# The last MLP group's down projection as seven block products for 12 of its 16 tiles

## The chip, the cores and the metric

The kernel runs on 1 core of one Trainium2 chip. The metric is the device time of one execution in microseconds, 2284.91 as the median of three (2282.47 to 2286.58).

## The reference

One layer, 512 tokens behind 16 meta tokens, width 2048, all in float32. The change touches only the last lines, the MLP and the final norm.

```python
    h_res = h_res + y
    h = rms_norm(h_res, norm_mlp_g[i])
    h_res = h_res + jnp.square(jax.nn.relu(h @ w_up[i])) @ w_down[i]
out = rms_norm(h_res, final_norm_g)
return out[:, N_META:]
```

`w_up` is 2048 x 8192, `w_down` 8192 x 2048.

## The kernel before

**Tiles.** Activations lie transposed, 128 features on the partitions and 512 tokens along the row; the output of the MLP is 16 tiles of 128 x 512 (`KT`). The hidden width is done in 8 groups of 1024 (`FFG`). A group has an up part (8 hidden tiles, `UT`, made in 4 pairs) and a down part that adds the group's share to all 16 tiles.

**Precision.** Each weight block (128 x 4 x 128, a "quarter") is split into a rounded high part, by ScalarE (`w_hi`), and a low rest, by VectorE (`w_lo`). Each product is three matmuls (`multiply`): high by high, high by low, low by high. Five slots of split blocks run ahead of TensorE (`RM`), and `quarter_used` counts the ones that TensorE is done with.

**Seven products.** In every down but the last, two output tiles (m and m + 8) times two halves of the tokens form a 2 x 2 block problem, and so do the halves of the hidden tiles. Seven products p1, p5, p6, p2, p4, p3, p7 of 12 matmuls with 256 columns take the place of eight. The operands are sums of blocks: `u_form` holds the seven forms of the activation (`uf0`, `uf1`, `uf2`), `w_sum` the sums of weight blocks. ScalarE copies partial results from PSUM to `part`, VectorE combines them into `delta`, and GpSimd adds `delta` to the residual in DRAM (`accum_op`, line 966). The `delta` buffers alternate between two.

**The last group before.** Its ups are made as whole rows (`u_whole`, `u_halves`), without forms. While they run, GpSimd loads the residual back (lines 971 to 973). The down is plain: first 16 tiles over hidden tiles 0 to 3 with 512 columns, then two passes, one for each half of the tokens, over hidden tiles 4 to 7. VectorE evacuates each tile into the residual (`last_res`). Behind each tile of the two passes ScalarE multiplies by the final gain (`nt1`), TensorE turns it (`turn_out`), ScalarE keeps it in `rows`. GpSimd squares each tile and sums the squares (`acc2`, lines 983 and 985), VectorE the last ones. Token sums (`sum_tokens`) give the norm of 256 tokens; the first half's rows are scaled and stored while the second half is still multiplied, the second half's rows at the end.

**What sets the order.** There is no planner: each engine's program is written out, and waits on semaphores link them. The functions: `last_group` on ScalarE and VectorE, the loop over `dense` on TensorE.

Of the kernel before, what the change touches and what calls it, by code (L numbers as in the profile page):

```python
# [31 lines left out]
P = 128  # L32
# [173 lines left out]
ORDER = [t // 2 + HALF_UT * (t % 2) for t in range(UT)]  # L206
# [36 lines left out]
def hybrid_layer(nc, x, meta, norm_mix_g, w_in, shift_mu, conv_w, decay_w0, decay_w2, iclr_a0, iclr_a2,  # L243
# [5 lines left out]
    res_dram = nc.dram_tensor("residual", [D, SEQ], F32, kind="Internal").ap()  # L249
    y_dram = nc.dram_tensor("mixed", [D, SEQ], F32, kind="Internal").ap()  # L250
# [222 lines left out]
    u_sq, u_hi_ready, u_ready = sem("u_sq"), sem("u_hi_ready"), sem("u_ready")  # L473
# [6 lines left out]
    res_back = sem("res_back")  # L480
# [152 lines left out]
    def _(sp):  # L633
# [123 lines left out]

        for m in range(KT):
            load_last(wdn_q[FFG - 1, 0, :, :, m, :], L_UP + m)
        for i in range(2 * KT):  # L760
            load_last(wdn_q[FFG - 1, 1, :, :, i % KT, :], L_UP + KT + i)
        for t in range(4):
            for h in range(2):
                sp.wait_ge(rows_scaled[h], (2, 4, 5, 6)[t])
# [6 lines left out]
    def _(pool):  # L771
# [199 lines left out]
        pool.dma_start(res_a[:], res_view[:, 0:7, :]).then_inc(res_back, 16)  # L971
        pool.dma_start(res_b[:], res_view[:, 7:14, :]).then_inc(res_back, 16)
        pool.dma_start(res_c, res_view[:, 14:16, :]).then_inc(res_back, 16)
        pool.wait_ge(quarter_used, Q_LAST)
        nc.gpsimd.memset(acc2[:], 0.0).then_inc(acc_step, 1)
        steps = ACC_STEPS + 1
        for h in range(2):
            cols = slice(h * NEAR, (h + 1) * NEAR)
            for m in range(KT - 1 - BY_DVE * h):
                n = T_HALF + h * KT + m  # L980
                pool.wait_ge(evacuated[n % 2], free(n))
                pool.wait_ge(acc_step, steps)
                nc.gpsimd.tensor_tensor(psq2[:, cols], last_res(m)[:, cols], last_res(m)[:, cols], ALU.mult).then_inc(acc_step, 1)  # L983
# [8 lines left out]
    def _(act):  # L992
# [396 lines left out]
        def last_group():  # L1389
# [22 lines left out]
            for i in range(2 * KT):  # L1412
# [7 lines left out]
                if i:  # L1420
                    keep_rows(i - 1)
# [1138 lines left out]
```

## Time and profile before

| | |
|---|---|
| median of three | 2284.91 us |
| profiled execution, own time | 2283.76 us |
| its span | 2282.0 us |
| TensorE busy | 2260.2 us, 99% |
| VectorE busy | 1694.0 us, 74% |
| ScalarE busy | 1110.6 us, 49% |
| GpSimd busy | 299.7 us, 13% |
| TensorE clock | 0.999 of full |

The span is the time from the first to the last instruction of one profiled execution. Busy shares are averages over it; which engine counts in a stretch is told by the waits there. PE is TensorE, DVE VectorE, ACT ScalarE, POOL GpSimd, SP SyncE.

### The profile page before, as it was taken

The numbers are of one execution on the slowest core, as the hardware profiler recorded it, in microseconds if no ns is written. First come the engines' busy times: TensorE is split into PE (matmuls) and PEld (weight loads), VectorE is DVE, ScalarE is ACT, GpSimd is POOL, SyncE is SP. The second block draws the span as 40 slices with busy tenths as digits, with TensorE's granted clock in tenths as the row PEclk, the third lists the DMA queues.
The fourth block names the chain that finished last, engine by engine and source line by source line (L and its number), as shares of the span: only waits on it lengthen the run. The fifth ranks groups of instructions, "written<-read, shape, count | busy, mean of one in ns | idle before, by whom it ended". The sixth has DMA issues, their size and how long they took to land.

```text
span 2282.0 us, 50606 instructions
## 1 busy us (share of the span) xinstructions
PE 2260.2 (99%) x19888; PEld 2109.2 (92%) x19888; DVE 1694.0 (74%) x2678; ACT 1110.6 (49%) x2076; POOL 299.7 (13%) x342
## 2 busy tenths in 40 slices
PE   8999999999999999999999999999999999999998
PEld 8999999999999788899999999999999999999888
DVE  7568577577586765588788778788788788787656
ACT  6534444344344423355555545555555455555436
POOL 5102012011020232200100001001001001001007
PEclk9999999999999999999999999999999999999999
DMA  8343343342442562535635636537447447357434
GB/s 253 82 107 83 95 97 85 94 109 70 110 96 81 148 188 81 173 104 136 159 102 138 140 102 157 140 91 166 123 111 167 120 113 170 97 132 196 140 102 153
DMA packets 513306, 286.07 MB, mean 125 GB/s; under 512 B 84526, under 2 KB 490544, under 8 KB 512688
## 3 DMA queue, kind: packets, MB, share of 16 engines
q1 hardware_dynamic: 478512, 224.19, 36.1%
q0 software_dynamic: 24080, 56.20, 11.2%
q10 hardware_dynamic: 10496, 2.62, 0.6%
q8 instruction: 155, 2.54, 0.5%
q14 instruction: 63, 0.52, 0.1%
HBM read 232.47 MB, written 50.47 MB: 124 GB/s over the span
## 4 chain that ended last, share of the span: by engine, by line
PE 91%; DVE 4%; DMA 2%; POOL 1%; ACT 1%; issue 1%; ACTq 0%; SPq 0%; POOLq 0%; DVEq 0%
PE PD L2152 17%; PE PD L2147 11%; PE PD L2402 10%; PE PD L2403 10%; PE PD L2404 10%; PE PW L2402 8%; PE PW L2403 8%; PE PW L2404 8%; PE PD L2368 1%; PE PD L2176 1%; PE PW L2176 1%; POOL acc L985 1%; PE PW L2226 1%; POOL psq L983 1%; DVE w_lo L1550 1%
## 5 line engine op out<-in xcount | busy, mean ns | idle before, releaser
L2152 PE MATMUL PD<-act_both,w_hi 128*128 128x264 f32 (+1 forms) x2496 | 412.7, 287 | 0.0
L2152 PEld LDWEIGHTS PD<-act_both,w_hi 128*128 128x128 f32 x2496 | 341.7, 188 | 11.5 <-issue 6.7
L2403 PE MATMUL PW<-uf,w_hi 128*128 128x256 f32 x1120 | 312.4, 279 | 0.0
L2402 PE MATMUL PW<-uf,w_hi 128*128 128x256 f32 x1120 | 312.4, 279 | 0.0
L2404 PE MATMUL PW<-uf,w_lo 128*128 128x256 f32 x1120 | 312.4, 279 | 0.0
L1036 ACT CAST w_hi<-w_sum 128x512 fp32r<-128x512 f32 x352 | 217.1, 617 | 181.2 <-PE PD L2404 121.2
L1503 DVE TENSOR_TENSOR w_lo<-w_sum,w_hi 128x512 fp32r<-128x512 f32 x352 | 240.4, 688 | 66.9 <-ACT w_hi L1036 65.1
L1550 DVE TENSOR_TENSOR w_lo<-w_raw,w_hi 128x512 fp32r<-128x512 f32 x268 | 200.5, 774 | 97.3 <-ACT w_hi L1052 93.8
L1052 ACT CAST w_hi<-w_raw 128x512 fp32r<-128x512 f32 x268 | 159.1, 619 | 209.4 <-DMA w_raw<-in_w_in 103.1
L2152 PE MATMUL PD<-act_both,w_lo 128*128 128x264 f32 (+1 forms) x1248 | 250.8, 282 | 0.0
L2403 PEld LDWEIGHTS PW<-uf,w_hi 128*128 128x128 f32 x1120 | 210.7, 188 | 0.3
L2402 PEld LDWEIGHTS PW<-uf,w_hi 128*128 128x128 f32 x1120 | 210.6, 188 | 0.3
L2404 PEld LDWEIGHTS PW<-uf,w_lo 128*128 128x128 f32 x1120 | 210.6, 188 | 0.0
L966 POOL DMA_DIRECT2D residual<-form x56 | 66.9, 1195 | 1063.4 <-DVE form L1978 950.6
L2403 PE MATMUL PD<-plain,w_hi 128*128 128x512 f32 x512 | 199.6, 390 | 0.0
L2402 PE MATMUL PD<-plain,w_hi 128*128 128x512 f32 x512 | 199.6, 390 | 0.0
L2404 PE MATMUL PD<-plain,w_lo 128*128 128x512 f32 x512 | 199.3, 389 | 0.0
L2152 PEld LDWEIGHTS PD<-act_both,w_lo 128*128 128x128 f32 x1248 | 191.4, 188 | 0.0
L1503 DVE TENSOR_TENSOR w_lo<-w_more,w_hi 128x512 fp32r<-128x512 f32 x212 | 141.9, 687 | 37.5 <-ACT w_hi L1036 37.3
L1301 ACT ACTIVATE part<-PW 128x256 f32<-128x256 f32 x264 | 101.1, 383 | 135.9 <-PE PW L2404 129.0
L1036 ACT CAST w_hi<-w_more 128x512 fp32r<-128x512 f32 x212 | 126.0, 617 | 67.2 <-PE PD L2404 39.4
L1036 ACT CAST w_hi<-w_raw 128x512 fp32r<-128x512 f32 x180 | 111.1, 618 | 80.6 <-PE PD L2404 36.0
(416 smaller groups left out, 5468.9 us busy)
## 6 DMA issues: line engine op xcount, KB each, us to landing
w_raw<-in_w_in SPq DMA_DIRECT2D x200, 256.0 KB, 3.1
w_raw<-in_w_down SPq DMA_DIRECT2D x136, 256.0 KB, 3.0
w_more<-in_w_down SPq DMA_DIRECT2D x136, 256.0 KB, 3.0
w_raw<-in_w_up SPq DMA_DIRECT2D x128, 256.0 KB, 3.1
w_more<-in_w_up SPq DMA_DIRECT2D x128, 256.0 KB, 3.3
residual<-form POOLq DMA_DIRECT2D x56, 512.0 KB, 7.5
w_raw<-in_w_out SPq DMA_DIRECT2D x64, 256.0 KB, 3.0
residual<-res POOLq DMA_DIRECT2D x2, 2048.0 KB, 10.1
```

The costliest lines, as they stand in the source:

```text
L966: pool.dma_start(res_view[:, p::HALF_KT, :], delta[:, p % 2].rearrange("p (a h) n -> p a (h n)", a=2), accum_op=ALU.add).then_inc(delta_ad ...
L1036: nc.scalar.copy(hi_slot(i), w_sum(SUM_IN[product]) if rel is None else raw_mlp(rel)).then_inc(hi_split, 1)
L1052: nc.scalar.copy(w_hi[:, q % RING], w_raw[:, q % RAW]).then_inc(hi_split, 1)
L1301: nc.scalar.activation(part[:, place, :], bank_for(product, unit) if bank is None else bank, ACT.Copy, scale=scale).then_inc(part_kept, 1)
L1503: V.tensor_tensor(lo_slot(i), w_sum(SUM_IN[product]) if rel is None else raw_mlp(rel), hi_slot(i).bitcast(F32), ALU.subtract).then_inc(lo_ ...
L1550: V.tensor_tensor(w_lo[:, q % RING], w_raw[:, q % RAW], w_hi[:, q % RING].bitcast(F32), ALU.subtract).then_inc(lo_split, 1)
L2147: ins = M(pd_seq(n)[:, 0:width], w, v[:, k, first:first + width], start=begin, stop=end)
L2152: ins = M(PD[:, 2 * (n % 2) + a, cols], w, v[:, k, start:start + cols.stop - cols.start], start=begin, stop=end)
L2176: ins = M(bank[:, h, cols], w, v[:, k, start:start + cols.stop - cols.start], start=begin, stop=end)
L2402: M(bank, whi, hi, start=begin, stop=False, skip_group_check=True)
L2403: M(bank, whi, lo, start=False, stop=False, skip_group_check=True)
L2404: return M(bank, wlo, hi, start=False, stop=end, skip_group_check=True)
```

## The change

The last group's ups go through the same code as the other groups, so that the seven forms are made. Its down is done by seven products for the tile pairs (0, 8) to (5, 13). The tiles 6, 14, 7, 15 (`END_TILES`) stay plain, in 8 steps: four tiles for the first half of the tokens, then four for the second, each over all eight hidden tiles with 256 columns.

Each pair is combined into `delta`, added to the residual in DRAM and loaded back into `res_pair`. Only then can its final gain, its transposes and its squares be made. ScalarE's gains (`gain_rows`) of pair p - 2 stand in pair p, TensorE's transposes behind p6 and p4. GpSimd squares a whole pair, 1024 columns, in one instruction (`pair_squares`). The squares of the end tiles are VectorE's. One block of each pair of hidden tiles (b12) is overwritten by forms, so GpSimd stores it in DRAM and loads it back for the plain end steps; ScalarE and VectorE round and split it again (`round_b12`, `low_b12`). The scaling of the first half's rows is done in whole rows, behind end steps 6 and 7.

The core of the diff:

```diff
+BY_SEVEN = 6
+END_TILES = [p + HALF_KT * x for p in range(BY_SEVEN, HALF_KT) for x in range(2)]
+UNITS = ([(p + HALF_KT * x, 0, 4) for p in range(BY_SEVEN) for x in range(2)]
+         + [(m, 2 * h, 2) for h in range(2) for m in END_TILES])
+AHEAD_OF_END = 8
+TURNED_BEHIND = ((8,), (9,), (), (), (10, 11, 12), (13, 14), (15, 16), (17, 18))
+SUM_BEHIND = 5
...
 gpsimd
-        pool.dma_start(res_a[:], res_view[:, 0:7, :]).then_inc(res_back, 16)
...
+        for u in range(HALF_UT):
+            pool.wait_ge(u_sq, UT * (FFG - 1) + 2 * u + 1)
+            pool.dma_start(b12_view[:, u, :], form[:, NP, :]).then_inc(b12_stored, 16)
+        pool.wait_ge(quarter_used, Q_DOWN)
+        for p in range(BY_SEVEN, HALF_KT):
+            pool.dma_start(res_pair(p), res_view[:, p::HALF_KT, :]).then_inc(res_back[2], 16)
+        pool.wait_ge(b12_stored, 16 * HALF_UT)
+        pool.dma_start(b12_back[:], b12_view).then_inc(b12_loaded, 16)
...
+        def pair_squares(p):
+            pool.wait_ge(res_back[p % 2], 16 * (p // 2 + 1))
...
+            nc.gpsimd.tensor_tensor(psq2[:], res_pair(p), res_pair(p), ALU.mult).then_inc(acc_step, 1)
+            pool.wait_ge(acc_step, steps[0] + 1)
+            nc.gpsimd.tensor_tensor(acc2[:], acc2[:], psq2[:], ALU.add).then_inc(acc_step, 1)
+        for p in range(BY_SEVEN):
+            pool.wait_ge(combined, COMBINED_0 + N_COMBINED * (HALF_KT * (FFG - 1) + p + 1))
+            pool.sem_inc(delta_taken, 1)
+            pool.dma_start(res_view[:, p::HALF_KT, :], delta[:, p % 2].rearrange("p (a h) n -> p a (h n)", a=2),
+                           accum_op=ALU.add).then_inc(delta_added[p % 2], 16)
+            pool.wait_ge(delta_added[p % 2], 16 * (1 + HALF_KT // 2 * (FFG - 1) + p // 2 + 1))
+            pool.dma_start(res_pair(p), res_view[:, p::HALF_KT, :]).then_inc(res_back[p % 2], 16)
+            if p:
+                pair_squares(p - 1)
+        pair_squares(BY_SEVEN - 1)
...
 scalar, in mlp_group's down
+                    if last and p >= 2 and i in (0, 2):
+                        gain_rows(2 * (p - 2) + i // 2)
+                    if last and p >= 2 and i in (4, 6):
+                        keep_rows(2 * (p - 2) + i // 2 - 2)
...
+        def gain_rows(u):
...
+                act.wait_ge(res_back[p % 2], 16 * (p // 2 + 1))
...
+            nc.scalar.activation(nt1[:, u % 3, 0:n * P], last_res(m)[:, t * P:(t + n) * P], ACT.Copy,
+                                 scale=p_("g_fin", m)).then_inc(gained, 1)
...
 vector
+            for e in range(END_STEPS):
...
+                end_split(2 * e + RM)
+                if e == 0:
+                    low_b12()
...
+                V.tensor_tensor(r, pd_seq(n)[:, 0:NEAR], r, ALU.add).then_inc(evacuated[n % 2], 1)
...
 tensor
+                    if last and p >= 2 and product in ("p6", "p4"):
+                        turn_out(2 * (p - 2) + (product == "p4"))
...
+        down(FFG - 1, BY_SEVEN, last=True)
+        pe.wait_ge(fin_kept, AHEAD_OF_END)
+        for e in range(END_STEPS):
+            h, n = e // len(END_TILES), T_PLAIN + e
+            if e >= 2:
+                pe.wait_ge(evacuated[n % 2], free(n) - 1)
...
+            for u in TURNED_BEHIND[e]:
+                turn_out(u)
+            if e == SUM_BEHIND:
+                pe.wait_ge(acc_step, ACC_STEPS + N_ACC)
...
+                sum_tokens(0, acc2[:, 0, 0:NEAR], acc2[:, 1, 0:NEAR], end_sq[:, 0, 0:NEAR], end_sq[:, 2, 0:NEAR])
```

GpSimd in the last group before, behind the adds of group 7: the residual comes back once, then squares of 256 columns follow each other.

```order
L966 DMA residual<-form 128x2x512 [waits combined]
L964 REGISTER_ALU
L966 DMA residual<-form 128x2x512 [waits combined]
L964 REGISTER_ALU
L966 DMA residual<-form 128x2x512 [waits combined]
L964 REGISTER_ALU
L966 DMA residual<-form 128x2x512 [waits combined]
L964 REGISTER_ALU
```

And GpSimd in the changed kernel, from the add of pair 2 on.

```order
L1015 DMA residual<-form 128x2x512 [waits combined]
L1018 DMA res_a<-residual 128x2x512 [waits delta_added0]
L1007 TENSOR_TENSOR psq<-res_a 128x1024 [waits acc_step,res_back_odd]
L1009 TENSOR_TENSOR acc<-acc,psq 128x1024 [waits acc_step]
L1015 DMA residual<-form 128x2x512 [waits combined]
L1018 DMA res_a<-residual 128x2x512 [waits delta_added1]
L1007 TENSOR_TENSOR psq<-res_a 128x1024 [waits acc_step,res_back_even]
L1009 TENSOR_TENSOR acc<-acc,psq 128x1024 [waits acc_step]
```

The add to DRAM, the load back and the squares of the pair before now stand in one queue, and the load waits for the add (`delta_added`).

ScalarE in the second pass before, where the first half's rows are scaled: `nt` is the gain, `w_hi` a split.

```order
L1046 CAST w_hi<-w_raw 128x512 [waits quarter_used,raw_loaded2]
L1418 ACTIVATE nt<-res_a,par 128x256 [waits fin_turned,evacuated0]
L1432 COPY rows<-PW 128x2x128 [waits fin_turned]
L1046 CAST w_hi<-w_raw 128x512 [waits quarter_used,raw_loaded3]
L1418 ACTIVATE nt<-res_a,par 128x256 [waits fin_turned,evacuated1]
L1432 COPY rows<-PW 128x2x128 [waits fin_turned]
L1444 ACTIVATE rows<-rows,rs_tok 128x512 [waits fin_kept,rs_ready]
```

ScalarE in the changed kernel, at the start of pair 2 of the last group's down (`part` copies are p1's, p5's and p6's).

```order
L1336 ACTIVATE part<-PW 128x256 [waits combined,quarter_used]
L1071 CAST w_hi<-w_sum 128x512 [waits quarter_used,sum_made]
L1442 ACTIVATE nt<-res_a,par 128x512 [waits res_back_even]
L1336 ACTIVATE part<-PW 128x256 [waits combined,quarter_used]
L1071 CAST w_hi<-w_sum 128x512 [waits quarter_used,sum_made]
L1336 ACTIVATE part<-PW 128x256 [waits combined,quarter_used]
L1071 CAST w_hi<-w_more 128x512 [waits quarter_used,raw_loaded4]
L1442 ACTIVATE nt<-res_a,par 128x512 [waits res_back_even]
```

The gain (`nt<-res_a`) waits for the load back, and the copies and splits stand behind it. ScalarE in the changed kernel, where the products end and the end tiles begin:

```order
L1081 CAST w_hi<-w_more 128x512 [waits quarter_used,raw_loaded4]
L1449 COPY rows<-PD 128x4x128 [waits fin_turned]
L1442 ACTIVATE nt<-res_b,par 128x512 [waits fin_turned,res_back_even]
L1081 CAST w_hi<-w_more 128x512 [waits quarter_used,raw_loaded5]
L1442 ACTIVATE nt<-res_b,par 128x512 [waits fin_turned,res_back_even]
L1449 COPY rows<-PW 128x4x128 [waits fin_turned]
L1081 CAST w_hi<-w_more 128x512 [waits quarter_used,raw_loaded6]
L1456 CAST uf<-b_back 128x2x256 [waits quarter_used,b12_loaded]
L1456 CAST uf<-b_back 128x2x256
```

A split stands ahead of the copy to `rows` that the end tiles wait for, and the gains of pair 4 (`nt<-res_b`, `res_back_even`) ahead of the rounding of the kept block.

## Rows read from the trace of the kernel before

**Rows 1.** Busy time by stretch: us, engines, TensorE clock, DMA share, GB/s.

```profile
core 0: us, PE busy (x) PEld busy (x) DVE busy (x) ACT busy (x) POOL busy (x), PEclk, DMA share, GB/s
2011.10:2089.40 78.30, 78.30 (x674) 78.30 (x673) 68.38 (x110) 45.26 (x92) 8.35 (x7) 1.00 0.65 150
2110.00:2174.20 64.20, 63.00 (x398) 56.78 (x398) 40.28 (x60) 30.59 (x57) 0.00 (x0) 1.00 0.46 139
2174.20:2271.40 97.20, 96.94 (x647) 88.68 (x645) 66.49 (x105) 52.25 (x112) 46.37 (x55) 1.00 0.40 122
```

**Rows 2.** Chain that ended last, last group: start, us, engine, tile, line.

```profile
2110.25 0.70 DVE form L1913
...
2131.59 0.70 DVE form L1913
...
2174.24 46.33 PE PD L2147 x216
2220.79 1.41 PE PD L2147 x12
2222.42 1.41 PE PD L2147 x12
```

**Rows 3.** VectorE in time, group 7: start, us, operation, idle time before.

```profile
1985.06 0.69 DVE L1913 TENSOR_TENSOR form<-PD,part 128x512 f32<-128x512 f32 x1 [1.39 <-PE PD L2404]
...
2005.77 0.69 DVE L1913 TENSOR_TENSOR form<-PD,part 128x512 f32<-128x512 f32 x1 [1.39 <-PE PD L2404]
...
2011.14 0.69 DVE L1913 TENSOR_TENSOR form<-PD,part 128x512 f32<-128x512 f32 x1 [0.21 <-PE PD L2404]
...
2023.58 0.68 DVE L1978 SCALAR_TENSOR_TENSOR form<-PW,part 128x512 f32<-128x512 f32 x1
```

**Rows 4.** GpSimd in time, group 7's down.

```profile
2024.89 1.19 POOL L966 DMA_DIRECT2D residual<-form  x1 [93.65 <-DVE form L1978]
...
2042.28 1.19 POOL L966 DMA_DIRECT2D residual<-form  x1 [8.01 <-DVE form L1978]
2052.07 1.20 POOL L966 DMA_DIRECT2D residual<-form  x1 [8.60 <-DVE form L1978]
```

**Rows 5.** DMA issues, KB each, us to landing: group 7, line 966, whole kernel.

```profile
residual<-form POOLq DMA_DIRECT2D x8, 512.0 KB, 7.2
...
DMA to landing us min/median/max: 6.3/7.5/9.1
...
yin<-mixed POOLq DMA_DIRECT2D x15, 256.0 KB, 3.5
...
res<-residual POOLq DMA_DIRECT2D x2, 1024.0 KB, 8.5
```

**Rows 6.** GpSimd by line: two with mean ns, two with ns min/median/max.

```profile
L983 POOL TENSOR_TENSOR psq<-res_a 128x256 f32<-128x256 f32 x14 | 10.6, 760 | 46.7 <-DVE res_a L2029 44.9
...
L973 POOL DMA_DIRECT2D form<-residual x1 | 0.7, 737 | 0.0
...
L946 POOL TENSOR_TENSOR psq<-res x15: 1030/1208/1257, 826.3 to 947.8; 128x512 f32 x14, 128x512 f32<-128x512 f32 x1
...
L948 POOL TENSOR_TENSOR acc<-acc,psq x15: 1281/1617/1624, 827.4 to 948.9; 128x512 f32<-128x512 f32 x15
```

**Rows 7.** ScalarE's groups by line and shape, last group's down and tail.

```profile
L1046 ACT CAST w_hi<-w_more 128x512 fp32r<-128x512 f32 x24 | 14.9, 621 | 20.9 <-PE PD L2147 18.0 <-PE PD L2404 2.1 <-DVE u_halves L1997 0.8
...
L1444 ACT ACTIVATE rows<-rows,rs_tok 128x1024 f32<-128x1024 f32 x2 | 2.2, 1140 | 0.2 <-DVE rs_tok L2052 0.2
```

**Rows 8.** Everything in time, around the last matmul.

```profile
2271.17 0.28 PE L2147 MATMUL PD<-u_halves,w_lo 128*128 128x256 f32 x1
...
2272.14 0.38 PE L2503 MATMUL PD<-ones,acc 128*128 128x1 f32 x2 [0.47 <-POOL acc L985]
...
2273.84 0.26 ACT L1437 ACTIVATE rs_tok<-PD,par 128x2 f32<-128x2 f32 x1
```

More of the change, by code:

```diff
@@ L1336, in keep_next, with mlp_group @@
             keep_up(u + 1, i, g) if u < HALF_UT - 1 else keep_down(0, i, g)
-        def mlp_group(g):
+        def mlp_group(g, pairs=HALF_KT, last=False):
             def square(u, x):
@@ L1379, in mlp_group @@
                         keep_next(u, 1, g)
-            for p in range(HALF_KT):
+            for p in range(pairs):
                 for i in range(NP):
@@ L1959, in mlp_group @@
                         V.tensor_tensor(t3, b22, b12, ALU.subtract).then_inc(form_made, 1)
-            for p in range(HALF_KT):
+            for p in range(pairs):
                 for i, product in enumerate(PRODUCTS):
@@ L2449, in up_pair, with down @@
                 ins.then_inc(quarter_used, 1)
-        def down(g):
+        def down(g, pairs=HALF_KT, last=False):
             whole = [(product, 0, KQ) for product in PRODUCTS]
@@ L2457, in down @@
             down_read = {"p1": -N_COMBINED, "p2": 1 - N_COMBINED, "p4": 0}
-            for p in range(HALF_KT):
+            for p in range(pairs):
                 for product, k0, k1 in whole if p else first:
@@ L2478, in down, with turn_out, sum_tokens @@
                         ins.then_inc(quarter_used, done)
+                    if last and p >= 2 and product in ("p6", "p4"):
+                        turn_out(2 * (p - 2) + (product == "p4"))
+        def turn_out(u):
+            m, first, n = UNITS[u]
+            pe.wait_ge(gained, u + 1)
+            if u < AHEAD_OF_END:
+                if u >= 2:
+                    pe.wait_ge(fin_kept, u - 1)
+            elif u >= AHEAD_OF_END + 4:
+                pe.wait_ge(fin_kept, u - 3)
+            else:
+                pe.wait_ge(combined, COMBINED_0 + N_COMBINED * (HALF_KT * (FFG - 1) + BY_SEVEN))
+            for t in range(n):
+                ins = nc.tensor.transpose(unit_bank(u)[:, t * P:(t + 1) * P], nt1[:, u % 3, t * P:(t + 1) * P], ident[:])
+            ins.then_inc(fin_turned, 1)
+        def sum_tokens(h, *parts, begin=True, end=True):
+            for t in range(2):
+                for i, squares in enumerate(parts):
+                    ins = M(PD[:, 1 + 2 * h, t:t + 1], squares[:, t * P:(t + 1) * P], ones2[:, 0:1],
+                            start=begin and t == i == 0, stop=end and i == len(parts) - 1, skip_group_check=True)
+            if end:
+                ins.then_inc(summed, 1)
         up_pair(0, 0, first=True)
```

367 lines of the change are left out of this document (174 added, 193 removed).

## The prediction

> **What bounds the kernel now.** The page's busy shares come first: TensorE leads, so what counts is its own work and every stretch in which it is kept waiting. The busy table by stretch [rows 1] shows group 7's down as a pattern (TensorE without a gap), and the three stretches that the change touches: the last group's ups (2110.0 to 2174.2, TensorE idle for 1.2), its down (2174.2 to 2271.4, 97.2 us), and the tail to 2282.0. The granted clock is 1.00, the upper level of 2.4 GHz, in each row. The chain of waits [rows 2] tells what is inside. In the ups each pair of tiles ends in a short detour over VectorE and ScalarE, since the new pair's first product waits for `part`. The down is TensorE itself, tile after tile; at its end GpSimd's squares are a little late and let the token sums start at 2272.14 [rows 8]. So TensorE has no gap to give back in the down; only fewer or cheaper matmuls help, and any wait longer than its cover is added in full.
>
> **Last group's ups: -1.9 us.** They take the code path of the other groups: products, forms, roundings. What that path costs TensorE is in VectorE's `form` rows of group 7 [rows 3]: 2005.77 - 1985.06 = 20.7 us per pair of tiles, no gap. Before, the last group has 2131.59 - 2110.25 = 21.34 us [rows 2]. Three such steps: 3 x 0.64 = 1.9 us gained. The four stores of the kept block (128 KB each) are issued by an idle GpSimd, and each is waited for some 20 us later: nothing. If a store were late VectorE would stand, with the weight splits queued behind it, but even the slowest of 56 adds of four times the size landed in 9.1 us [rows 5]. SyncE loads 40 weight blocks instead of 48 in the down, from a queue of its own: nothing.
>
> **Last group's down, without waits: -8.0 us.** Before: 192 matmuls of 512 columns. The piece of 46.33 us holds them and two 12-matmul steps of 1.41 [rows 2]: (46.33 - 2.82)/192 = 0.227 us each, 43.5 us. Then 384 of 256 columns at 1.41/12 = 0.1175: 45.1. A step returns every 1.63 us, so two transposes take 0.22: 64 of them 7.0. Token sums and the wait before them add about 1.6, which gives the 97.2 to within 0.1. After: a pair of down tiles by products returns to GpSimd's issue every 52.07 - 42.28 = 9.8 us [rows 4], 84 matmuls at 0.1167. Six pairs 58.8, 8 end steps of 24 matmuls 22.4, and what of the transposes and sums lies ahead of the last matmul 3.5 + 2.9 + 1.6. That is 89.2 us with no wait, against 97.2 before; the rest of this part is the waits.
>
> **The new round trip: +11.4 us.** A pair's `delta` goes combined -> GpSimd add to DRAM -> landed -> load back -> ScalarE gain -> TensorE transpose. GpSimd's queue does this in order, and waits for each add before it goes on. Its prices: add, from issue to landing, 7.2 us (median of group 7's eight; 6.3 to 9.1 over 56) [rows 5]. Load back of 512 KB: 256 KB take 3.5, 1024 KB queued behind another 8.5 [rows 5]; bounds 3.5 and 5.5, I take 4.4, nearer the short one, because nothing is queued ahead of it. Its issue holds GpSimd 0.75 (row of `form<-residual`, the same 512 KB) [rows 6]. Squares of 1024 columns: at 512 the product takes 1.03 to 1.26, median 1.21, the sum 1.28 to 1.62, median 1.62; at 256 the product's mean is 0.76 [rows 6], so a fixed part of 2 x 0.76 - 1.21 = 0.3 stands in each. Doubled less 0.3: 2.1 and 2.9 to 3.0, together 5.1 us; bounds 4.1 (fastest, less 0.3 each) and 5.8 (slowest, doubled). One turn of GpSimd's loop is then 7.2 + 0.75 + 5.1 + 0.3 for semaphores = 13.3 us, while TensorE makes a pair in 9.8 + 0.9 of transposes = 10.7. GpSimd falls behind. At 512 columns the sum's median is its slowest, 1.62, beside a busy VectorE. The Trainium skill (GPSIMD Engine Reference, section 3.1) gives about 2.6 cycles of 1.2 GHz per element for a two-input operation, an estimate of 2.2 us for 1024 columns, and section 8 adds that VectorE instructions with two SBUF inputs contend for the same interfaces. By the first alone the loop would be 12.6 and the kernel some 3 us faster than I say; the slower rows agree with the second.
>
> Walk, in us from the down's first matmul. Pair 0's combination is late, as in group 7: VectorE's row is at 2023.58, 12.4 after the ups' end at 2011.14 [rows 3], and GpSimd's issue at 2024.89, 13.8 after [rows 4]. Add 0 lands at 21.0, its load at 25.5, gain (0.75 for 512 columns, where ScalarE takes 1.14 for 1024 [rows 7]) 26.3. TensorE wants it behind p6 of pair 2: 19.6 + 4.2 = 23.8. Wait 2.5. Behind the standing gain ScalarE has the copy of p5 and the split two products on; p3 and p7 need them, so they bite later than TensorE's own wait at p6. Pair 2 ends at 32.7. Add 2 is issued at 34.6, from here GpSimd sets the pace: adds at 34.6, 47.9, 61.2, 74.5. Pair 3 and 4 find their loads in time (33.7 for 36.9, 46.2 for 47.6). Pair 5 wants load 3 at 58.3 and gets it gained at 60.4: 2.2. It ends at 66.9. The end tiles first wait for the eighth unit to be kept, and ScalarE puts a split ahead of that copy: 0.62 [rows 7] and as much for the copy, with semaphores 1.5. End step 0 ends at 71.2, but unit 8's gain (load 4 at 72.9) is ready at 73.7: 2.5. The late ScalarE delays the rounding of the kept block, VectorE's `low_b12` stands ahead of step 0's evacuation, and step 2 needs that bank: 0.7. Units 10 to 12 (load 5 at 86.2): 1.3. Squares of pair 5 end at 92.8 where token sums could begin at 92.1: 0.7. Sum: 2.5 + 2.2 + 1.5 + 2.5 + 0.7 + 1.3 + 0.7 = 11.4. Last matmul at 89.2 + 11.4 = 100.6, against 97.2.
>
> **Tail: +0.4 us.** Before, 2.4 us lie between the last matmul and `root_tokens` at 2273.84 [rows 8], 0.5 of it GpSimd's lateness. That goes. Late instead is ScalarE: two full-row scalings of 1.14 [rows 7] stand ahead of the last gains, unit 18's transposes wait about 0.9. I count 2.8. Behind the root nothing changes: two scalings of 1024 columns per engine and four stores. The stores of rows 0 and 1 move towards the tail, but are issued 5 us ahead of the last rows'.
>
> **Sum.** -1.9 + 3.4 + 0.4 = +1.9 us. The profiled execution took 2283.76 (span 2282.0), 1.15 under the median; with it 2285.7, from the median 2284.91 I forecast 2286.8, written 2287. A difference under 0.2% (4.6 us) counts as none.
>
> **VectorE** has room: group 7's down keeps it busy 68.4 of 78.3 us [rows 1], 8.5 of the 9.8 us of a pair. A pair now lasts 10.7, and beside GpSimd its work would have to grow by a quarter before it held the products: nothing.
>
> **Rivals.**
> - *The round trip stays hidden* (time about 2278.5, 0.3% faster). For it: loads of 3.5, adds of 6.3 and squares of 4.1 are the bounds, the loop is then 11.4 and only pair 2 (0.6), the 1.5 and the 0.4 stay with about 1 more: 89.2 + 3.1 - 97.2 = -4.9, less 1.9, plus 0.4: -6.4. Against: group 7's adds averaged 7.2, and VectorE runs nearly through. 14%.
> - *GpSimd decides it alone* (slower): its loop reaches 14.6 us, with squares at 5.8 and adds at 7.8. Add 5 starts 3 x 1.3 later, its landing 0.7 and the load 1.1 later, pair 2 waits 1.8 more: 7.5 us, time about 2294. It is slower than 0.2% from a loop of about 13.9. For it: the sum's median at 512 columns is near its slowest [rows 6], and the adds' own median over all groups is 7.5 [rows 5]; against, group 7's 7.2. With the upper part of my own case, 36%.
> - *The load back is short.* The time of one load as a mechanism: every gain, and both end waits, come earlier by what the load is shorter. With 3.5 instead of 4.4 pair 2 resumes 0.9 sooner, and with it every later add, and the last load lands 0.9 sooner again: 1.8 in all, 2285. 12%, inside the 50% below. The Trainium skill (DMA: Bandwidth & Descriptors, section Anatomy of one DMA) fits 2.0 us plus bytes over 436 GB/s for a DMA from this queue, 3.2 us for 512 KB as an estimate, which would give 2284.5; the adds' 7.2 us don't follow it.
>
> **How the numbers follow.** Within 0.2%: 50%, my sum and its near neighbours. Faster 14%, slower 36%. The range for 8 in 10 runs from 2279 (loop near 12) to 2295 (loop near 14.8); my own case alone is 2282 to 2291.
>
> **What would show it.** GpSimd's adds should be 13 us apart from pair 2 on and its squares about 2.1 and 3.0 us. TensorE should wait for `nt` at pair 2, pair 5, behind end step 0 and behind step 4, some 8 to 9 us together, and 1.5 for the eighth `rows` copy. The last ups should be 20.7 us apart. I am wrong if adds follow TensorE at 10 to 11 us (then faster), or if VectorE, not GpSimd, holds the products.

## The result: 13.4 us slower, outside the range

The changed kernel takes 2297.41 us (median of 5, 2293.75 to 2301.92), the kernel before, beside it, 2283.97 (2282.47 to 2286.58). The ratio is 1.0057, interval 1.0045 to 1.0069: slower by more than 0.2%, where 2287 (2279 to 2295) was forecast, and no change held half of the chance. The profiled execution took 2297.64 us, its span 2295.5, that is 13.5 more than before.

The busy table by stretch of the changed kernel, to be read against [rows 1]: the last group's ups, its down, the tail.

```profile
core 0: us, PE busy (x) PEld busy (x) DVE busy (x) ACT busy (x) POOL busy (x), PEclk, DMA share, GB/s
2110.00:2173.00 63.00, 63.00 (x402) 57.16 (x401) 49.91 (x83) 32.30 (x64) 1.64 (x3) 1.00 0.37 107
2173.00:2284.00 111.00, 95.76 (x772) 94.10 (x771) 85.27 (x117) 61.37 (x122) 38.01 (x26) 0.95 0.56 144
2284.00:2295.50 11.50, 2.61 (x23) 2.29 (x21) 3.10 (x6) 4.66 (x9) 0.00 (x0) 0.73 0.90 357
```

The ups have lost their idle time. All of the loss is in the down, where TensorE works 95.8 of 111 us and the mean granted clock is 0.95. From its first matmul to its last it takes 2283.82 - 2172.95 = 110.9 us; before it was 97.1, and 100.6 was forecast. What TensorE waited for from the down's first matmul to the end (in total, times, longest; before only one wait of 0.5 us stood there, behind the last matmul):

```profile
PE PD L2456 <- DVE res_b L2088: 6.3, 3, 4.8
PE PD L2548 <- ACT nt L1442: 5.0, 3, 3.1
PE PW L2548 <- ACT nt L1442: 3.2, 2, 2.7
PE PD L2456 <- ACT rows L1449: 1.2, 1, 1.2
```

0.6 us of the `nt` row in PW stand behind the last matmul, so TensorE idles 15.2 us in the down. The two rows of `nt` (7.7 us of it) and the row of `rows` are waits that the walk named. The largest was not in it at that size: the end tiles' products wait 6.3 us for VectorE's evacuation at L2088, 4.8 of it ahead of end step 4. Read what VectorE did there, and GpSimd beside it. VectorE in time (start, us, operation; x2 is two instructions in one row):

```profile
2253.94 0.43 DVE L2073 TENSOR_TENSOR end_sq<-res_b 128x256 f32<-128x256 f32 x1
2254.28 3.50 DVE L1614 TENSOR_TENSOR w_lo<-w_more,w_hi 128x512 fp32r<-128x512 f32 x2
2257.71 0.41 DVE L2088 TENSOR_TENSOR res_b<-PD,res_b 128x256 f32<-128x256 f32 x1
2258.15 2.16 DVE L2073 TENSOR_TENSOR end_sq<-res_b 128x256 f32<-128x256 f32 x1
2260.34 2.01 DVE L2098 TENSOR_TENSOR end_sq<-end_sq 128x256 f32<-128x256 f32 x1
2262.27 3.43 DVE L1614 TENSOR_TENSOR w_lo<-w_raw,w_hi 128x512 fp32r<-128x512 f32 x2
2265.63 0.41 DVE L2088 TENSOR_TENSOR res_b<-PD,res_b 128x256 f32<-128x256 f32 x1
```

GpSimd in the same stretch, pair 4's and pair 5's squares:

```profile
2255.31 1.91 POOL L1007 TENSOR_TENSOR psq<-res_b 128x1024 f32<-128x1024 f32 x1
2257.30 2.72 POOL L1009 TENSOR_TENSOR acc<-acc,psq 128x1024 f32<-128x1024 f32 x1
2260.18 1.90 POOL L1007 TENSOR_TENSOR psq<-res_b 128x1024 f32<-128x1024 f32 x1
2262.15 2.40 POOL L1009 TENSOR_TENSOR acc<-acc,psq 128x1024 f32<-128x1024 f32 x1
```

One and the same instruction, L2073 on 256 columns, takes 0.43 us at 2253.94 and 2.16 at 2258.15. The second ends at 2260.31, where GpSimd's addition ends (2260.02), the one behind it at 2262.35, where the next ends (2262.08). In these rows a VectorE instruction that reads two SBUF operands lasts until the GpSimd instruction beside it is over; I call this the hold. L2088, whose one operand is in PSUM, takes 0.41 throughout. The Trainium skill (GPSIMD Engine Reference, section 8, Key points) states that GpSimd shares its SBUF interfaces with VectorE and contends with instructions that have two SBUF inputs; the trace agrees, with 1.7 us added to an instruction of 0.43.

GpSimd's issues of the adds to DRAM, against [rows 4]:

```profile
2186.86 1.21 POOL L1015 DMA_DIRECT2D residual<-form  x1 [11.46 <-DVE form L2050]
...
2195.13 1.19 POOL L1015 DMA_DIRECT2D residual<-form  x1 [0.20 <-issue]
...
2210.64 1.22 POOL L1015 DMA_DIRECT2D residual<-form  x1 [4.10 <-DVE form L2050]
...
2224.52 1.22 POOL L1015 DMA_DIRECT2D residual<-form  x1
...
2235.97 1.23 POOL L1015 DMA_DIRECT2D residual<-form  x1
...
2248.43 1.22 POOL L1015 DMA_DIRECT2D residual<-form  x1
```

From the first matmul on: 13.9, 22.2, 37.7, 51.6, 63.0, 75.5. Forecast were 13.8, 22, 34.6, 47.9, 61.2, 74.5. The last three gaps are 13.9, 11.5 and 12.5 us, where 13.3 was forecast.

Last, TensorE's clock, in stretches of 4 us (columns as above):

```profile
2192.00:2196.00 4.00, 4.00 (x37) 4.00 (x36) 3.63 (x7) 1.54 (x4) 1.62 (x2) 1.00 0.86 198
2196.00:2200.00 4.00, 0.91 (x8) 0.71 (x7) 0.00 (x0) 0.75 (x2) 0.32 (x1) 1.00 0.90 252
2200.00:2204.00 4.00, 3.97 (x21) 3.97 (x22) 3.08 (x5) 2.74 (x6) 0.14 (x1) 0.57 0.73 136
2204.00:2208.00 4.00, 4.00 (x36) 4.00 (x36) 3.87 (x5) 2.05 (x5) 2.52 (x2) 1.00 0.36 131
...
2260.00:2264.00 4.00, 1.26 (x11) 1.06 (x9) 3.96 (x3) 2.42 (x4) 3.77 (x3) 1.00 0.01 3
2264.00:2268.00 4.00, 1.91 (x9) 1.91 (x10) 3.93 (x7) 0.00 (x0) 0.56 (x1) 0.66 0.00 0
2268.00:2272.00 4.00, 4.00 (x20) 4.00 (x20) 2.59 (x6) 1.03 (x2) 0.00 (x0) 0.50 0.00 0
```

In the 4 us behind the wait of 3.1 us at 2196.9 the mean clock is 0.57, behind the one of 4.8 us at 2261.3 it is 0.66 and then 0.50, the lower level of 1.2 GHz: 20 matmuls in 4 us, not 37. In the down 56 steps from one product to the next take over 0.15 us where 0.117 is usual, 5.8 us in excess. Some 1.5 of it is there at full clock too (15 such steps in the down of the kernel without the round trip and with the other banks, below, at clock 1.00); the other 4.3 us are the clock.

### The profile page after: what moved, and what is told of

It is laid out like the page before. It is cut to its first block, busy times and chain, and to the rows that moved or that the text cites. A ratio compares the mean times of both kernels' runs of the same rounds, so it can differ in the third digit from the quotient of the medians.

```text
span 2295.5 us, 50882 instructions
## 1 busy us (share of the span) xinstructions
PE 2258.8 (98%) x20020; PEld 2114.7 (92%) x20020; DVE 1723.0 (75%) x2713; ACT 1122.9 (49%) x2094; POOL 290.9 (13%) x314
## 4 chain that ended last, share of the span: by engine, by line
PE 87%; DVE 7%; DMA 3%; issue 2%; POOL 1%; ACT 1%; ACTq 0%; SPq 0%; DVEq 0%; POOLq 0%
PE PD L2206 16%; PE PD L2456 10%; PE PD L2457 10%; PE PD L2458 10%; PE PD L2201 8%; PE PW L2456 8%; PE PW L2457 8%; PE PW L2458 8%; PE PD L2422 1%; PE PD L2230 1%; PE PW L2230 1%; DVE w_lo L1618 1%; PE PW L2381 1%; DMA w_raw<-in_w_in 1%; PE PW L2280 1%
## 5 line engine op out<-in xcount | busy, mean ns | idle before, releaser
L2206 PEld LDWEIGHTS PD<-act_both,w_hi 128*128 128x128 f32 x2496 | 341.7, 188 | 11.5 <-issue 6.7
L2456 PE MATMUL PW<-uf,w_hi 128*128 128x256 f32 x1240 | 346.1, 279 | 0.0
L2457 PE MATMUL PW<-uf,w_hi 128*128 128x256 f32 x1240 | 345.7, 279 | 0.0
L2458 PE MATMUL PW<-uf,w_lo 128*128 128x256 f32 x1240 | 345.7, 279 | 0.0
L1071 ACT CAST w_hi<-w_sum 128x512 fp32r<-128x512 f32 x376 | 231.9, 617 | 191.3 <-PE PD L2458 126.9
L1571 DVE TENSOR_TENSOR w_lo<-w_sum,w_hi 128x512 fp32r<-128x512 f32 x376 | 260.8, 699 | 72.6 <-ACT w_hi L1071 71.4
L1087 ACT CAST w_hi<-w_raw 128x512 fp32r<-128x512 f32 x268 | 159.2, 619 | 212.4 <-DMA w_raw<-in_w_in 113.7
L2457 PEld LDWEIGHTS PW<-uf,w_hi 128*128 128x128 f32 x1240 | 233.2, 188 | 0.3
L2456 PEld LDWEIGHTS PW<-uf,w_hi 128*128 128x128 f32 x1240 | 233.1, 188 | 0.3
L2458 PEld LDWEIGHTS PW<-uf,w_lo 128*128 128x128 f32 x1240 | 233.1, 188 | 0.0
L1336 ACT ACTIVATE part<-PW 128x256 f32<-128x256 f32 x282 | 108.2, 384 | 140.2 <-PE PW L2458 132.4
L1571 DVE TENSOR_TENSOR w_lo<-w_more,w_hi 128x512 fp32r<-128x512 f32 x221 | 151.4, 704 | 31.2 <-ACT w_hi L1071 30.8
L2456 PE MATMUL PD<-uf,w_hi 128*128 128x256 f32 x560 | 159.2, 284 | 7.6 <-DVE res_b L2088 6.3
## 6 DMA issues: line engine op xcount, KB each, us to landing
residual<-res POOLq DMA_DIRECT2D x2, 2048.0 KB, 10.3
```

Source lines behind the costliest of these rows:

```text
L1071: nc.scalar.copy(hi_slot(i), w_sum(SUM_IN[product]) if rel is None else raw_mlp(rel)).then_inc(hi_split, 1)
L1087: nc.scalar.copy(w_hi[:, q % RING], w_raw[:, q % RAW]).then_inc(hi_split, 1)
L1336: nc.scalar.activation(part[:, place, :], bank_for(product, unit) if bank is None else bank, ACT.Copy, scale=scale).then_inc(part_kept, 1)
L1571: V.tensor_tensor(lo_slot(i), w_sum(SUM_IN[product]) if rel is None else raw_mlp(rel), hi_slot(i).bitcast(F32), ALU.subtract).then_inc(lo_ ...
L2206: ins = M(PD[:, 2 * (n % 2) + a, cols], w, v[:, k, start:start + cols.stop - cols.start], start=begin, stop=end)
L2456: M(bank, whi, hi, start=begin, stop=False, skip_group_check=True)
```

## Experiments

The hold theory: the loss comes from GpSimd's arithmetic on the squares, by holding VectorE and by delaying the next transfer (in the expectations this second part is called pace, and is the rival of the first). Its rivals: the round trip through DRAM alone (add, landing, load back, landing) sets the pace, or the lower clock does. Medians of the kernel before were 2283.85 beside the first four kernels, 2284.01 beside the next four, 2284.49 beside the last three.

**Narrow squares.** `pair_squares` in pieces of 256 columns, so that one hold is shorter.

```diff
-            pool.wait_ge(acc_step, steps[0])
-            nc.gpsimd.tensor_tensor(psq2[:], res_pair(p), res_pair(p), ALU.mult).then_inc(acc_step, 1)
+            for a, cols in pieces:      # 2 x 2 pieces of 256 columns
+                r = res_pair(p)[:, a, cols]
+                pool.wait_ge(acc_step, steps[0])
+                nc.gpsimd.tensor_tensor(psq2[:, a, cols], r, r, ALU.mult).then_inc(acc_step, 1)
```

> GpSimd's pair squares in instructions of 256 columns instead of 1024 (four times as many, same data, same place in its queue). Theory 'hold': a VectorE instruction with two SBUF operands ends only when the GpSimd tensor_tensor beside it ends, so in the changed kernel it is held for up to 1.9 or 2.7 us. Then the longest VectorE split falls from 2.8 to about 1.3 us, TensorE's wait of 4.8 us for the evacuation in the end tiles falls under 1.5, and the clock stays at 1.00 there: 5 to 7 us faster than the changed kernel, 2291 to 2293, with adds no closer together. Theory 'pace' (only GpSimd's loop of 12 to 13 us counts): the loop grows by the extra instructions, time 2297 to 2300.

Measured: 2300.38 us, ratio 1.0072 (1.0056 to 1.0089). The 2291 to 2293 of the hold was missed; the time lies just above the 2297 to 2300 of the pace. GpSimd's groups by shape (busy us, mean ns), then TensorE's two largest waits:

```profile
L1012 POOL TENSOR_TENSOR acc<-acc,psq 128x256 f32<-128x256 f32 x20 | 17.8, 888 | 1.6
L1010 POOL TENSOR_TENSOR psq<-res_a 128x256 f32<-128x256 f32 x12 | 9.1, 758 | 0.8
```

```profile
PE PD L2551 <- ACT nt L1445: 8.6, 3, 5.2
PE PD L2558 <- POOL acc L1012: 5.2, 1, 5.2
```

Half of the expectation did come true. The holds shrank (`w_lo<-w_sum` means 765 ns, in the changed kernel 880; VectorE is busy 76.0 us from 2174 to 2290, not 87.6), and no wait for the evacuation is left. But four pieces take 3.0 and 3.6 us where one whole takes 1.9 and 2.7, and GpSimd's arithmetic grew from 24.3 to 35.2 us. The work between two transfers grew, adds 3 to 5 came at 2227.29, 2239.87, 2254.10, the last 5.7 us later than in the changed kernel, and TensorE waited for the gains and for the last squares instead.

**No squares, and memsets in their place.** Both kernels leave the squares of the twelve tiles out of the token sums, so their output is not the reference's. The first keeps one memset, for pair 0. The second puts 5 memsets of the same tile there for each pair (2 for pair 0), each waited for, which keep GpSimd about as long.

```diff
-            nc.gpsimd.tensor_tensor(psq2[:], res_pair(p), res_pair(p), ALU.mult).then_inc(acc_step, 1)
-            pool.wait_ge(acc_step, steps[0] + 1)
-            nc.gpsimd.tensor_tensor(acc2[:], acc2[:], psq2[:], ALU.add).then_inc(acc_step, 1)
+            for n in range(2 if p == 0 else 5):        # the second kernel alone
+                nc.gpsimd.memset(acc2[:], 0.0).then_inc(acc_step, 1)
```

> GpSimd makes no pair squares at all (the squares of the 12 tiles are left out of the token sums). Both hold and pace are gone: adds follow TensorE at 10 to 11 us, no VectorE split over 0.7 us. What stays are the waits at pair 2 (3.1 us with its slow clock after it, 1.7), the 1.2 for the eighth kept unit and perhaps 1 at the first end steps. Both theories: 2281 to 2284, 14 to 16 us faster than the changed kernel. If it stays above 2290, the round trip itself is the cost and neither theory holds.

> Memsets of 1024 columns stand where the squares stood, two for a product and three for a sum (squares of the 12 tiles left out), so GpSimd's loop keeps its length of 12 to 13 us but it reads nothing from SBUF. Theory 'hold': VectorE runs free (no split over 0.9 us), the waits from pace stay (pair 2, end step 0, units 10 to 12): 2289 to 2292. Theory 'pace': as the changed kernel, 2296 to 2298. If a memset holds VectorE too, its instructions show 1.0 us and more.

Measured: without squares 2284.14 us, ratio 1.0000 (0.9990 to 1.0010); with memsets 2289.70, ratio 1.0023 (1.0013 to 1.0033). The first is at the upper end of its band, the second inside the hold's and far from the pace's. With memsets GpSimd is as busy as with squares (25.9 us against 24.3), and VectorE isn't held:

```profile
L1566 DVE TENSOR_TENSOR w_lo<-w_sum,w_hi 128x512 fp32r<-128x512 f32 x22 | 14.8, 687 | 18.5 <-ACT w_hi L1066 18.5
...
L1003 POOL MEMSET acc<- 128x1024 f32 x27 | 25.9, 958 | 1.3
```

So of the changed kernel's 13.4 us, 7.7 go with the hold (2297.41 to 2289.70) and 5.6 more with GpSimd's time (to 2284.14). By the intervals of the ratios each of the two is uncertain by 3 to 4 us. The memsets' loop is also somewhat longer than that of the squares (adds 14.6, 12.6 and 13.6 us apart, against 13.9, 11.5 and 12.5), so the hold's share is rather more than 7.7. And with memsets TensorE waits for no evacuation at all, where it waited 6.3 us. What is left of the changed kernel's waits without squares:

```profile
PE PD L2542 <- ACT nt L1436: 3.9, 1, 3.9
PE PD L2450 <- ACT rows L1443: 1.2, 1, 1.2
PE PW L2542 <- ACT nt L1436: 1.0, 2, 0.6
PE PD L2450 <- DVE res_b L2082: 0.4, 1, 0.4
```

**Squares ahead of the landing wait.** Squares of pair p - 1 behind add p's issue, while that add is under way.

```diff
+            if p:
+                pair_squares(p - 1)
             pool.wait_ge(delta_added[p % 2], 16 * (1 + HALF_KT // 2 * (FFG - 1) + p // 2 + 1))
             pool.dma_start(res_pair(p), res_view[:, p::HALF_KT, :]).then_inc(res_back[p % 2], 16)
-            if p:
-                pair_squares(p - 1)
```

> The squares of pair p-1 stand behind the issue of add p and ahead of the wait for its landing, still 1024 columns each. GpSimd's loop becomes as long as TensorE's pair, 10 to 11 us; VectorE is held as long as before, but earlier. Theory 'pace' : waits at end step 0 and at units 10 to 12 go, 2289 to 2291. Theory 'hold': the splits held up in the pairs stay, but the end tiles are beside fewer squares, 2291 to 2295.

Measured: 2292.55 us, ratio 1.0038 (1.0028 to 1.0047), inside the hold's band and above the pace's. GpSimd's time is hidden behind the landings (add 5 at 2246.65, 1.8 us earlier than in the changed kernel), the hold stays (`w_lo` up to 3.17 us). That is 2.9 us above the memsets and 8.4 above no squares. Not all of it need be the hold: in the profiled execution one load back took 7.5 us to land, and TensorE waited 5.3 us for the gain behind it.

**The clock.** The kernel without squares, with 32 matmuls whose result is thrown away in pair 2's wait.

```diff
+                    if last and p == 2 and product == "p6":
+                        for _ in range(32):
+                            M(PD[:, 0, 0:NEAR], u_form(1, 0)[:, 0, 0:P], u_form(0, 0)[:, 0, :], start=True, stop=True)
                     if last and p >= 2 and product in ("p6", "p4"):
                         turn_out(2 * (p - 2) + (product == "p4"))
```

> As e2_none (squares of the kept residual left out, so GpSimd only starts transfers and takes the low halves), with 32 further matmuls of 256 columns whose result is thrown away, put ahead of the transposes of pair 2's product p6, where TensorE idled 3.9 us in e2_none. The clock theory (the granted clock falls to .57 in 2200 to 2204 because TensorE stood idle, and the matmuls behind it are slower by 1.7 us for it): the filled stretch ends at the same time, the granted clock of the stretch behind it stays at 1.00, and the time is 1.5 to 2 us below e2_none, about 2282.4. The rival, that the clock falls with the work and not with the idle time, or that what follows is paced by GpSimd's transfers anyway: no change, 2284 (within 0.5).

Measured: 2284.83 us, ratio 1.0001 (0.9991 to 1.0010): no gain, as the rival says. The clock itself did what the clock theory says; the row without squares, then the row with the filling:

```profile
2200.00:2204.00 4.00, 2.69 (x13) 2.69 (x14) 1.80 (x2) 2.91 (x6) 0.00 (x0) 0.57 0.96 175
```

```profile
2200.00:2204.00 4.00, 3.61 (x32) 3.41 (x30) 1.82 (x2) 2.92 (x6) 0.00 (x0) 1.00 0.84 149
```

In the profiled executions the down is 1.5 us shorter (97.7 against 99.2), in the medians of 10 runs there is no gain. The idle time lets the clock fall; that this costs the kernel its 1.7 us isn't shown. What follows may be paced by the transfers, as the rival has it; that reason is not tested, and neither is the fall behind the evacuation in the changed kernel.

**Squares on ScalarE, sums on VectorE.**

```diff
+        def square_pair(p):
+            act.wait_ge(res_back[p % 2], 16 * (p // 2 + 1))
+            ...
+            nc.scalar.activation((psq2 if p else acc2)[:], res_pair(p), ACT.Square).then_inc(pair_squared, 1)
+        def add_pair(p):
+            ...
+            V.tensor_tensor(acc2[:], acc2[:], psq2[:], ALU.add).then_inc(acc_step, 1)
```

> The squares of the twelve kept tiles taken by ScalarE (one activation of 1024 a pair, estimate 1.1 us each) and their sums by VectorE (one addition of 1024 a pair, estimate 0.7 to 1.2 us each), so GpSimd only starts transfers; nothing is left out. The hold theory (after's loss is GpSimd's arithmetic, half by holding VectorE and half by pacing the round trips): as e2_none plus at most 3 us, 2284 to 2287; low halves never longer than 0.70 us on VectorE; adds issued as in e2_none, the sixth about 71 us behind the first down matmul. The rival, that VectorE's or ScalarE's queue cannot take six more instructions of this length without TensorE waiting for splits: 2289 or more, with TensorE's waits for the low halves grown beyond 2 us in sum.

Measured: 2287.82 us, ratio 1.0019 (1.0010 to 1.0029), 0.8 above the band and 9.6 below the changed kernel, with nothing left out; the low halves take 687 ns and TensorE waits for none. Its waits are 3.4 us for `nt` in PD, 1.2 for `rows`, 1.0 for the sums.

**Pair 2's transposes two products later**, and then **the kept units on the other banks**, so that the first end step waits for the seventh unit to be kept and not for the eighth. Both start from the kernel with squares on ScalarE.

```diff
-                    if last and p >= 2 and product in ("p6", "p4"):
+                    if last and p > 2 and product in ("p6", "p4"):
                         turn_out(2 * (p - 2) + (product == "p4"))
+                    if last and p == 2 and product in ("p4", "p7"):
+                        turn_out(product == "p7")
```

```diff
-        return PD[:, 2 * (u % 2), :] if u < AHEAD_OF_END else PW[:, u % 4, :]
+        return PD[:, 2 * ((u + 1) % 2), :] if u < AHEAD_OF_END else PW[:, u % 4, :]
...
-        pe.wait_ge(fin_kept, AHEAD_OF_END)
         for e in range(END_STEPS):
+            if e < 2:
+                pe.wait_ge(fin_kept, AHEAD_OF_END - 1 + e)
```

> f1_act with pair 2's gains and transposes two products later (behind p4 and p7 instead of p6 and p4), so that pair 0's round trip has about 4.9 us more. If pair 2's wait is the rest of the loss: the wait of 3.9 us goes to under 0.5, the granted clock behind it stays at 1.00 (1.7 us more), nothing else moves: 4 to 5.5 us below f1_act, 2279 to 2282. The rival, that this time is given back at pair 3 because the GpSimd queue (add, landing, load back, landing) takes as long as a pair's products: under 2 us below f1_act, with the wait at pair 3 or 4 in its place.

> f2_later with the units of the kept part on the other PSUM banks, so that the first step of the end waits for the seventh unit kept and not the eighth. Expected: TensorE's wait of 1.2 us for the rows kept by ScalarE goes, 1 us below f2_later. The rival: step 0's next wait is for the end's first low half and takes its place, no change within 0.3 us.

Measured: 2286.04 us (ratio 1.0010, 1.0000 to 1.0019) and 2286.32 (1.0013, 1.0003 to 1.0022). The first gained 1.8 us, not 4 to 5.5: the rival, with part of the time given back at later pairs. TensorE's waits for `nt` in PD:

```profile
PE PD L2561 <- ACT nt L1439: 3.3, 3, 1.4
```

The waits of 2.5 and 0.8 us have become three, of 1.4, 0.5 and 1.4. The second removed the wait for `rows` and won nothing, as its rival says.

**No round trip.** Squares on ScalarE as above; the residual is loaded ahead, and VectorE adds `delta` on chip. Then the same with the other banks.

```diff
         for p in range(BY_SEVEN):
-            pool.wait_ge(combined, COMBINED_0 + N_COMBINED * (HALF_KT * (FFG - 1) + p + 1))
-            pool.dma_start(res_view[:, p::HALF_KT, :], ..., accum_op=ALU.add).then_inc(delta_added[p % 2], 16)
-            pool.wait_ge(delta_added[p % 2], 16 * (1 + HALF_KT // 2 * (FFG - 1) + p // 2 + 1))
+            pool.wait_ge(combined, COMBINED_0 + N_COMBINED * (HALF_KT * (FFG - 1) + p))
             pool.dma_start(res_pair(p), res_view[:, p::HALF_KT, :]).then_inc(res_back[p % 2], 16)
+        def add_delta(p):
+            dve.wait_ge(res_back[p % 2], 16 * (p // 2 + 1))
+            ...
+            V.tensor_tensor(r, delta[:, p % 2].rearrange("p (a h) n -> p a (h n)", a=2), r, ALU.add).then_inc(res_made, 1)
```

> f1_act without the round trip: the residual of a kept pair is loaded on chip ahead of the pair's products' end, and VectorE adds delta to it there (one addition of 1024 columns a pair, estimate 1.1 to 1.3 us); no add goes to DRAM; squares on ScalarE and their sums on VectorE as in f1_act. Nothing is left out. If what remained of the loss in f1_act and f2_later was the round trip (TensorE's waits for nt, 3 to 4 us, and the lower clock behind them, 1 to 2 us): these go, 1.25 us for the eighth unit's rows and about 1 for the sums remain, the down takes 92 to 94 us and the time is 2279 to 2282, under before. The rival, that VectorE is full: six more instructions of over 1 us turn into waits of the products for the low halves, 2285 or more.

> g1_chip with the units of the kept part on the other PSUM banks, so that step 0 of the end waits for the seventh unit kept and not the eighth. Expected: 1.25 us of TensorE's wait for rows goes and g1_chip's time falls by about 1 us. The rival, as in f3_bank, which gave nothing: the next wait takes its place, within 0.3 us of g1_chip.

Measured: 2281.88 us, ratio 0.9989 (0.9980 to 0.9998), and with the other banks 2278.58, ratio 0.9976 (0.9967 to 0.9985). The only change against the kernel with squares on ScalarE is the round trip, and it is worth 5.9 us (2287.82 to 2281.88). Both beat the kernel before, the first by 2.6 us, which is under the 0.2% that counts here, the second by 5.9 us. The second's down takes 91.6 us from first to last matmul, at clock 1.00, in a profiled execution that is one of its two fastest (2276.65); its waits:

```profile
PE PD L2569 <- DVE acc L2065: 1.0, 1, 1.0
PE PW L2562 <- ACT nt L1431: 0.6, 1, 0.6
```

The banks, worth nothing with the round trip (2286.04 to 2286.32), are worth 3.3 us without it (about 1 was expected): a wait is only worth its length where no later one takes it back. In the profiled executions 1.25 is the wait, and some 1.4 are slow matmuls in the first kernel's 2260 to 2268 (clock 0.84 and 0.74), which the second doesn't have.

**The hold alone.** The changed kernel's squares stay on GpSimd, without the round trip.

```diff
         def pair_squares(p):
-            pool.wait_ge(res_back[p % 2], 16 * (p // 2 + 1))
+            pool.wait_ge(res_made, p + 1)
...
-            if p:
-                pair_squares(p - 1)
+            if p > 1:
+                pair_squares(p - 2)
```

> The changed kernel with its squares and sums left on GpSimd, but without the round trip: residual loaded ahead, delta added on chip by VectorE as in g1_chip. GpSimd's arithmetic no longer stands between a transfer and the next, so its pace can delay nothing; what is left of it is the hold. Hold theory: VectorE's low halves beside the squares still last up to 2.9 us, VectorE's busy time from 2174 to 2290 is some 10 us or more above g1_chip's, TensorE waits for the low halves, and the time is 2285 to 2291, 5 to 9 us above g1_chip. The rival, that only the pacing of the round trips cost time and VectorE's longer instructions are hidden: within 2 us of g1_chip.

Measured: 2294.48 us, ratio 1.0041 (1.0026 to 1.0057): 12.6 us above the same kernel with squares on ScalarE. The hold theory had the sign and too small a size (5 to 9 us), its rival (within 2 us) is out. VectorE is fuller here than in the changed kernel, since it adds `delta` too, so the 12.6 us are not the hold's price there. VectorE's groups, and TensorE's largest wait:

```profile
L1568 DVE TENSOR_TENSOR w_lo<-w_sum,w_hi 128x512 fp32r<-128x512 f32 x22 | 23.8, 1102 | 0.0
L2063 DVE TENSOR_TENSOR res_a<-form,res_a 128x1024 f32<-128x1024 f32 x4 | 9.2, 2312 | 0.0
```

```profile
PE PW L2464 <- DVE w_lo L1568: 5.3, 5, 1.6
```

The same in the kernel with squares on ScalarE:

```profile
L1562 DVE TENSOR_TENSOR w_lo<-w_sum,w_hi 128x512 fp32r<-128x512 f32 x22 | 14.9, 684 | 0.9 <-ACT w_hi L1052 0.9
...
L2059 DVE TENSOR_TENSOR res_a<-form,res_a 128x1024 f32<-128x1024 f32 x4 | 4.9, 1217 | 0.0
```

VectorE is busy 98.9 of the 116 us from 2174 to 2290, against 83.0, of which 6.1 were sums that this kernel leaves to GpSimd: 22.0 us of hold beside 25 us of GpSimd arithmetic. In the changed kernel it is 17.4 us (87.6, with memsets 70.2) beside 24.3.

## Why the prediction was wrong

Spans add up: the down's first matmul 2172.95 instead of 2174.08 (-1.1), the down 110.9 instead of 97.1 (+13.8), from its last matmul to the end of the span 11.7 instead of 10.8 (+0.9), together +13.5. Forecast was +1.9, with +3.4 in the down.

- **Last group's ups, -1.9.** Right in the mechanism. VectorE's `form` rows, as in [rows 3]:

```profile
2111.03 0.69 DVE L1981 TENSOR_TENSOR form<-PD,part 128x512 f32<-128x512 f32 x1 [0.18 <-PE PD L2458]
...
2131.74 0.69 DVE L1981 TENSOR_TENSOR form<-PD,part 128x512 f32<-128x512 f32 x1 [0.18 <-PE PD L2458]
```

  They are 20.71 apart. The execution as a whole ran 0.8 late by then (group 7's row at 2006.55, not 2005.77), so the down began only 1.1 earlier.
- **Down without waits, 89.2.** 1.4 too little. The best kernel (no round trip, other banks) needs 91.6 with 1.0 of idle time: 90.6. Its 15 steps at full clock of about 0.2 us instead of 0.117 come to as much.
- **Waits, 11.4.** TensorE idles 15.2 us in the down. Pair 2's wait came at 3.1 (forecast 2.5), the eighth unit's at 1.2 (1.5), the one behind end step 0 at 2.7 (2.5). The other `nt` waits are 1.1 at pair 4 and 0.7 at pair 5 (2.2 forecast at pair 5 alone), and those behind step 4 and for the squares (1.3 and 0.7) don't appear: 8.9 in all where 10.7 was forecast. "Step 2 needs that bank: 0.7" is where it failed: the waits for the evacuation are 6.3, 0.4 at step 2, 1.1 at step 3 and 4.8 at step 4. Ahead of the L2088 of step 2 stand two splits, a square, a sum and two splits, and they were held to 3.5, 2.2, 2.0 and 3.4 us.
- **The failed step** is therefore "beside GpSimd its work would have to grow by a quarter before it held the products: nothing". It weighed VectorE's load as a mean over a pair. A hold comes in one piece, in the few microseconds in which GpSimd's two instructions run, and there VectorE's work grew threefold (2254.28 to 2265.70, 11.4 us, for instructions of 1.28, 0.41, 0.43, 0.43 and 1.28 us). One of the prediction's own signs of being wrong, "if VectorE, not GpSimd, holds the products", is what came. The prediction had named the contention, and used it only to price GpSimd's own instructions (2.1 and 3.0; measured 1.9 and 2.4 to 2.7). Taking the hold away with memsets was worth 7.7 us.
- **The kernel before showed the hold already.** There GpSimd's squares and sums of 256 columns take 46 us of the down, and VectorE's splits beside them mean 0.80 us and reach 1.14, where 0.69 is usual:

```profile
L1546 DVE TENSOR_TENSOR w_lo<-w_more,w_hi 128x512 fp32r<-128x512 f32 x24 | 19.2, 799 | 2.8 <-ACT w_hi L1046 2.2
```

  That is some 4.6 us over 44 splits, and TensorE waited for none of them. The change did not bring the hold, it made each piece two to three times as long and put it where VectorE was late. VectorE was late there because ScalarE's splits stood behind pair 4's gains: it had idled 6.1 us up to 2250.21.
- **Clock, not named.** 4.3 us of slow steps in the profiled execution, some 1.7 behind pair 2's wait and the rest behind the evacuation's. As the filled kernel shows, not all of that need come back in time if it were removed.
- **Tail, +0.4.** From the last matmul's end to `root_tokens` it took 3.1 us, where 2.8 was counted.
- **The rival *GpSimd decides it alone*** (2294) was near in time for a reason that isn't the one given: its loop was not 14.6 but 11.4 to 13.9 us from pair 2 on. *The load back is short* is out: 4.1 to 5.5 us, median 4.7, where 4.4 was taken and 3.5 was the rival's.
- **Where the expected gain went.** The products by seven save 6.5 of the 8.0 us counted (90.6 us of down without waits in the best kernel, against 97.1). With the round trip that is not to be seen: without any squares on GpSimd the kernel is where it was (1.0000). Without the round trip, and with the squares on ScalarE, it is 2.6 to 5.9 us faster than before.

Together: 1.4 (matmuls) + 3.8 (waits: 5.6 more for the evacuation, 1.8 less for the others) + 4.3 (clock) is 9.5 of the 10.3 us by which the down missed its forecast; 0.8 is not accounted for.

## What to carry to other kernels

Before GpSimd gets arithmetic beside a busy VectorE, list VectorE's instructions with two SBUF operands in that stretch, and add up to the whole of GpSimd's duration to one of them each time (17 of 24 us and 22 of 25 here; with pieces of 256 columns 5.9 of 35): then ask what is queued behind it. Price it by the stretch, not by the mean load. Cutting the pieces smaller shortens the hold but lengthens GpSimd's own work, so it helps only where nothing waits for GpSimd. A result that has to pass through DRAM and back can be paid in waits at the far end even where each transfer looks hidden; where the other operand can be loaded ahead, one VectorE addition (1.2 us a pair here) is cheaper than add and load back, 7.1 and 4.7 us to their landings.

## What the runs showed that I had not expected

- A GpSimd `tensor_tensor` holds a VectorE instruction with two SBUF operands to its own end: 0.43 to 2.16 us at 256 columns, 0.68 to 2.9 at 512; 22 us of hold for 25 us of GpSimd work. A memset of the same tile holds nothing (`w_lo` at 687 ns), and an instruction whose one operand is in PSUM isn't held (0.41).
- GpSimd's instructions lengthen too: in the kernel with narrow squares the product of 256 columns takes 0.61 us while VectorE idles and up to 0.99 beside it, the sum 0.72 and up to 1.60.
- GpSimd pays for small pieces: 256 columns took 758 and 888 ns on the mean, 1024 took 1.9 and 2.7 us, so that four pieces cost 1.3 to 1.6 times the whole. Part of that is VectorE: where it idles, 4 x 0.61 against 1.91 and 4 x 0.72 against 2.36 make 1.2 to 1.3.
- The length of a wait doesn't tell by itself whether the clock falls. After 3.1 us without a matmul the granted clock was 0.57 in the next 4 us, after a wait of 2.7 us at 2247 it stayed at 1.00; but with narrow squares it was 0.61 in the 4 us behind a wait of 2.3, and with squares on ScalarE it stayed at 1.00 behind one of 2.5 and was at 0.74 and 0.50 from 2260 to 2268, around a wait of 1.0 at 2260.3.
- Open: what the lower clock costs in time, and whether the last group's ups or its down alone would gain; neither was run apart.
